# Two transformer blocks on one core: gain vectors by ScalarE's queue, the first weights in quarters, and three changes of order

## The chip, the core and the metric

One core of a Trainium2 chip runs the whole program in one launch. TensorE multiplies matrices and writes PSUM, VectorE, ScalarE and GpSimd (POOL in the profile) work on SBUF and, but for GpSimd, on PSUM; SyncE (SP) and ScalarE (ACT) issue transfers, each on a queue of its own. The engines run their own instruction streams in order and meet in semaphores. The metric is the device time of one execution in microseconds, the median of several.

## The reference

A layer on 256 tokens of width 1024, in fp32, made of two blocks. The first:

```python
h = rms_norm(x, g_norm); proj = h @ w_in        # q_a k_a v_a q_i k_i w_i z_a c_q c_kv k_rope z_b q_m z_m gates
o_a = dsa_attention(q_a, k_a, v_a, q_i, k_i, w_i)         # 8 heads of 64, the 64 best keys of an index score
o_b = causal_attention(q_b, k_b, v_b)                     # 8 heads of 96, from the latents c_q, c_kv
o_m = softmax(q_m @ k_m.T) @ v_m                          # 4 heads of 128, keys and values: rms_norm(mem) @ w_mem_kv
x = x + (sum_n sigmoid(gate_n) * ((o_n * silu(z_n)) @ w_branch[n])) @ w_out
```

The second block has three residual steps: a mixer (differential attention "DA", 4 heads, beside a chunked gated linear attention "GLA", whose inputs are `q * e_pos`, `q * e_neg` and `k * exp(L_end - L)`, both through w_o), a cross attention "C" of 4 heads of 256 over a second memory (w_cq, w_ckv, w_co), and a mixture of 32 experts, two for each token, with w_e_gate, w_e_up and w_e_down (201 MB of weights in all).

## The kernel before, in words

Everything is written out by hand: each engine's stream is one function body, and the order in it is the schedule. Tokens lie in two tiles of 128 (`t`), a width of 1024 in 8 slices of 128 (`k`).

**Weights** come in chunks of up to 2 MB. `chunks` lists them; SyncE's stream (from L1148) issues them in this order into a ring of three slots, each behind the last product that read the slot (`wait_full`, L1157). Ahead of the first chunk it issues mem, the nine `gains` (small vectors that all end in one 55 x 128 tile GR) and the positions. The first chunk, mk, is split into two halves; TensorE waits for the first on `first_landed`, for the rest before slice 4. The 20 vectors of `small` follow the fourth chunk. After the last chunk come the router's weights and the experts' stream: 96 loads of 2 MB into eleven places, each behind the work that frees its place (L1180 to L1212); from load 13 on every second one goes by ScalarE's queue (L1679).

**Projections.** `project` (L513) and `project_t` multiply a turned activation by a chunk, 512 or 256 columns at a time; an fp32 matmul shows as two records. `project_blocks` (L646) multiplies by blocks with 7 products in place of 8 (28 matmuls); GpSimd's `weight_sums` (L1302) makes the four sums of weight blocks for it, S_a, S_b, then w21 and w12 in place, four instructions each, and VectorE's `combine` (L1845) adds the products up as `block_products` counts them. `project_rows` (L553) does one token tile and half at a time. The argument `after` is a function that is called behind every matmul and may put other work there.

**Transposes.** `turn` (L576) transposes four 128 x 128 pieces through an AUX bank of PSUM; ScalarE (`drain_turned`, L1426) or, with a gain, VectorE (`drain_rows`, L1752) takes them out. There are four AUX banks; `wait_drained` waits until a bank was taken out. At the start (L722 to L732) TensorE transposes three tiles of mem, then GR, then the fourth, waits for all four drains and starts mk.

**Attention.** `attend` on TensorE, `soften` on ScalarE and `attention` on VectorE run the same steps s = 0, 1, ...: in step s TensorE computes the scores of unit s, transposes the probabilities of unit s-2 and multiplies unit s-3 by the values; VectorE masks unit s (scaling and row maximum), normalizes unit s-1 and takes the output of unit s-3; ScalarE does the exponentials of unit s, then copies the transposed probabilities of unit s-2. `spread` (L685) lays TensorE's steps evenly between the matmuls of a projection: all eleven steps of the first attention, "A" with 8 units, lie in chunk zb, behind its seventh matmul; qm follows. ScalarE does tanh of zb, VectorE `silu_t` of zb, behind their last step of A.

**GLA.** GpSimd's stream (from L1368) runs the weight sums of gv and ckv1, waits for the decays' exponentials, makes the three products QP, QN and KE (L1374 to L1376, counted by `gla_products`) and then the weight sums of gg. TensorE waits for `gla_products` behind gg, before it transposes KE; ScalarE waits for it before the tanh of gg.

**Cross attention.** wcq is computed in four pieces (t, h) (L921 to L938). For each ScalarE squares and drains the bank, VectorE norms it. TensorE transposes the keys xk ahead of piece (1, 0) and the queries of tile 0 ahead of (1, 1). ScalarE drains xk and the first queries behind its drain of piece (1, 0). `start_sum` (L940) adds x3 into an ACC bank through the identity, half by half; then come the four units of C and the output weights wco (`add_wco`), whose results let the last loads of the experts' first groups go (`x3_done`).

## Time and profile before

| | us |
|---|---|
| runs (3), lowest, median, highest | 1123.66, 1124.64, 1125.01 |
| the profiled execution | 1124.0 |
| its span | 1122.2 |
| TensorE busy, share of the span | 925.8, 83% |
| VectorE busy | 404.1, 36% |
| GpSimd busy | 247.3, 22% |
| ScalarE busy | 170.3, 15% |
| HBM read | 288.51 MB |

Times in the views count from the span's start. TensorE's busy time is that of its records, whose ends are modelled. "PEclk" is the clock granted to TensorE as a share of the full 2.4 GHz. An idle time in brackets stands before an instruction, with what ended it behind the arrow.

### The profile page before, as it was taken

What the parts mean: (1) busy time and instruction counts of PE and PEld (TensorE: products, weight loads), DVE (VectorE), ACT (ScalarE), POOL (GpSimd) and SP (SyncE); (2) the same over time, 40 slices, a digit from 0 to 9 for tenths busy, and PEclk for the clock granted to TensorE, in tenths of its full rate; (3) what the DMA queues carried; (4) which work ended last, traced back from release to release, by engine and by line L of the source; (5) the groups of instructions that cost most, each with busy time, mean ns of one, the idle gap of its engine ahead of it and who ended that gap; (6) DMA issues with size and microseconds to landing.
All of it is one profiled execution on the core that took longest, in us unless ns stands there. A gap on an engine that the chain in (4) does not pass through costs nothing.

```text
span 1122.2 us, 12455 instructions
## 1 busy us (share of the span) xinstructions
PE 925.8 (83%) x5006; PEld 581.2 (52%) x5006; DVE 404.1 (36%) x984; ACT 170.3 (15%) x370; POOL 247.3 (22%) x368
## 2 busy tenths in 40 slices
PE   6999999999999999989999999655656557473847
PEld 3775487789999878865544555221211213131312
DVE  5537935762223655866545424010000101010101
ACT  2114232431001003013312311000000000000000
POOL 4543141234753948930000000000000000000000
PEclk9999999999999999999999999887786978687889
DMA  7636242224445344524219458999999999999997
GB/s 281 195 121 225 80 145 76 76 76 150 154 170 208 109 152 155 203 93 150 79 71 350 180 225 371 425 429 428 428 428 428 426 428 428 428 428 428 429 421 276
DMA packets 64312, 290.38 MB, mean 259 GB/s; under 512 B 9015, under 2 KB 11902, under 8 KB 52222
## 3 DMA queue, kind: packets, MB, share of 16 engines
q1 hardware_dynamic: 58206, 205.16, 47.6%
q10 hardware_dynamic: 6048, 84.41, 17.7%
q8 instruction: 41, 0.67, 0.2%
q14 instruction: 17, 0.14, 0.0%
HBM read 288.51 MB, written 1.05 MB: 258 GB/s over the span
## 4 chain that ended last, share of the span: by engine, by line
PE 56%; DMA 29%; DVE 5%; POOL 5%; ACT 2%; issue 2%; SPq 1%; another core or an unknown queue 1%; DVEq 0%; ACTq 0%; POOLq 0%
PE ACC L530 11%; DMA ring<-in_w_e_down_dram 10%; DMA PJ<-in_w_e_down_dram 10%; PE ACC L545 8%; PE ACC L668 7%; PE ACC L671 7%; PE ACC L569 5%; DMA BIG<-in_w_e_gate_dram 4%; DMA ring<-in_w_e_gate_dram 4%; POOL ring L1298 4%; PE AUX L1097 4%; PE AUX L1061 3%; PE ACC L953 2%; PE AUX L580 2%; PE AUX L700 1%
## 5 line engine op out<-in xcount | busy, mean ns | idle before, releaser
L1298 POOL TENSOR_TENSOR ring<-ring 128x256 f32<-128x256 f32 x272 | 204.5, 782 | 173.7 <-PE ACC L668 72.4
L1061 PE MATMUL AUX<-ring,R 128*32 128x512 f32 x400 | 132.7, 716 | 41.8 <-DMA BIG<-in_w_e_up_dram 20.7
L545 PE MATMUL ACC<-BIG,ring 128*128 128x256 f32 (+1 forms) x464 | 106.2, 382 | 0.0
L545 PEld LDWEIGHTS ACC<-BIG,ring 128*128 128x128 f32 (+1 forms) x464 | 84.6, 187 | 15.6 <-issue 3.6
L2305 DVE SCALAR_TENSOR_TENSOR GB<-GB,AUX 128x512 f32<-128x512 f32 x8 | 5.5, 688 | 235.0 <-ACT GB L1683 235.0
L1061 PE MATMUL AUX<-R 128*32 128x512 f32 x176 | 60.7, 707 | 25.6 <-DMA ring<-in_w_e_up_dram 11.0
L1061 PE MATMUL AUX<-BIG,R 128*32 128x512 f32 x176 | 64.0, 737 | 20.3 <-DMA PJ<-in_w_e_up_dram 20.3
L1097 PE MATMUL AUX<-ring,BIG 128*32 128x512 f32 x160 | 60.2, 707 | 21.9 <-DMA R<-in_w_e_down_dram 12.3
L530 PE MATMUL ACC<-ring,BIG 128*128 128x512 f32 (+2 forms) x192 | 76.0, 554 | 0.0
L1061 PE MATMUL AUX<-SQE,R 128*32 128x512 f32 x112 | 61.6, 713 | 16.9 <-DMA ring<-in_w_e_up_dram 9.8
L1061 PEld LDWEIGHTS AUX<-ring,R 128*32 128x32 f32 x400 | 31.4, 129 | 76.0 <-issue 76.0
L671 PE MATMUL ACC<-ring 128*128 128x256 f32 x288 | 64.2, 380 | 5.0 <-POOL ring L1298 4.1
L530 PE MATMUL ACC<-ring,R 128*128 128x512 f32 (+1 forms) x136 | 59.9, 589 | 3.2 <-DVE R L1758 2.1
L671 PEld LDWEIGHTS ACC<-ring 128*128 128x128 f32 x288 | 54.5, 190 | 13.5 <-POOL ring L1298 4.9
L1061 PE MATMUL AUX<-PJ,R 128*32 128x512 f32 x160 | 51.1, 697 | 7.0 <-DMA ring<-in_w_e_up_dram 7.0
L569 PE MATMUL ACC<-ring,BIG 128*128 128x512 f32 x128 | 55.8, 592 | 0.0
L2307 DVE SCALAR_TENSOR_TENSOR GB<-GB,AUX 128x512 f32<-128x512 f32 x8 | 8.4, 1049 | 129.9 <-PE AUX L1061 129.9
L530 PEld LDWEIGHTS ACC<-ring,BIG 128*128 128x128 f32 x192 | 36.2, 190 | 36.2 <-issue 28.4
L1097 PE MATMUL AUX<-PJ,BIG 128*32 128x512 f32 x128 | 45.0, 724 | 11.4 <-DMA ring<-in_w_e_down_dram 11.4
L668 PE MATMUL ACC<-ring 128*128 128x128 f32 x384 | 44.7, 275 | 0.0
L668 PEld LDWEIGHTS ACC<-ring 128*128 128x128 f32 x384 | 44.1, 192 | 0.2
L671 PE MATMUL ACC<-ring,R 128*128 128x256 f32 x184 | 42.2, 388 | 0.0
(345 smaller groups left out, 1422.3 us busy)
## 6 DMA issues: line engine op xcount, KB each, us to landing
ring<-in_w_in_dram SPq DMA_DIRECT2D x20, 2048.0 KB, 7.9
ring<-in_w_e_gate_dram SPq DMA_DIRECT2D x8, 2048.0 KB, 39.2
ring<-in_w_e_up_dram SPq DMA_DIRECT2D x6, 2048.0 KB, 41.9
ring<-in_w_e_gate_dram ACTq DMA_DIRECT2D x6, 2048.0 KB, 27.8
ring<-in_w_e_down_dram SPq DMA_DIRECT2D x5, 2048.0 KB, 40.1
ring<-in_w_e_up_dram ACTq DMA_DIRECT2D x5, 2048.0 KB, 24.2
ring<-in_w_ckv_dram SPq DMA_DIRECT2D x4, 2048.0 KB, 8.1
BIG<-in_w_e_down_dram SPq DMA_DIRECT2D x4, 2048.0 KB, 21.7
```

The source lines that it names most:

```text
L530: mm = nc.tensor.matmul(bank[:, t * 512:t * 512 + width], lhs[:, i, t * P:(t + 1) * P], w[:, i, a:a + width], start=(i == 0), stop=(i == k ...
L545: mm = nc.tensor.matmul(bank[0:m, j * S:(j + 1) * S], w[:, i, a + j * P:a + j * P + m], rhs[:, i, :], start=(i == 0), stop=(i == k - 1))
L569: mm = nc.tensor.matmul(bank[:, c:c + 512], lhs[:, i, t * P:(t + 1) * P], w[:, i, :], start=(i == order[0]), stop=(i == order[-1]))
L580: mm = nc.tensor.transpose(bank[0:src.shape[1], j * P:(j + 1) * P], src, ident[:, :])
L668: mm = nc.tensor.matmul(bank[:, j * P:(j + 1) * P], left[:, k, j * P:(j + 1) * P], right[:, k, :], start=(k == 0), stop=(k == 3))
L671: mm = nc.tensor.matmul(bank, right[:, k, :], left[:, k, :], start=(k == 0), stop=(k == 3))
L700: return lambda o, t, h, i, nk: nc.tensor.matmul(o, queries(t, h, i), keys(h, i, nk), start=True, stop=True)
L953: mm = nc.tensor.matmul(ACC[t][:, h * 512:(h + 1) * 512], XT3[:, i, t * P:(t + 1) * P], slot_of(f"wco{h}")[:, i, :], start=False, stop=Fal ...
L1061: mm = nc.tensor.matmul(bank[r, :], M_xt[:, k, r], w[e][:, k, :], start=(k == 0), stop=(k == KD - 1))
L1097: mm = nc.tensor.matmul(AUX[2 + h][r, :], M_hidt[:, k, r], w[e][:, k, h * 512:(h + 1) * 512], start=(k == 0), stop=(k == 3))
L1298: ins = g.tensor_tensor(out[:, k, :], a[:, k, :], b[:, k, :], op)
L2307: v.scalar_tensor_tensor(out=permuted, in0=M_gated.rearrange("q (p k) -> q p k", k=4), scalar=0.5, in1=AUX[3][:, :].rearrange("q (p k) -> ...
```

## The change

Only the order, the queues and the split of one load change; the arithmetic stays.

- The nine gain vectors and the positions are issued by ScalarE's queue, at the head of its stream, instead of SyncE's between mem and mk.
- mk's first half is loaded in two parts of two slices each, with a semaphore each.
- TensorE transposes the gains first, then all of mem, and mk waits for a mem drain only ahead of the four slices that need it.
- Steps 0 to 5 of the first attention are spread over zb, steps 6 to 10 lie behind matmuls 5, 10, 15, 20 and 25 of qm. ScalarE and VectorE do tanh and silu of zb behind their step 5, and VectorE combines qm in four parts between its later steps.
- GpSimd makes gg's weight sums ahead of the GLA products.
- In the cross attention ScalarE drains xk behind wcq's piece (0, 1); the second `start_sum` is done in halves, one ahead of the last queries' transposes and one behind unit 1's scores; and in attention C ScalarE copies the transposed probabilities ahead of the exponentials of the same step.

```diff
--- before.py
+++ after.py
@@ -208,7 +208,7 @@
         pos_landed = sem("pos_landed")
-        first_landed = sem("first_landed")
+        first_landed = [sem(f"first_landed{i}") for i in range(2)]
         x_landed = sem("x_landed")
@@ -513,9 +513,7 @@
-                if name == "mk":
-                    pe.wait_ge(first_landed, 16)
-                else:
+                if name != "mk":
                     wait_chunk(name)
@@ -523,8 +521,13 @@
                     for i in range(k):
-                        if (name, t, i) == ("mk", 0, 4):
-                            wait_chunk(name)
+                        if name == "mk":
+                            if i % 4 == 0:
+                                wait_drained(pe, ("mem", t, i // 4))
+                            if t == 0 and i in (0, 2):
+                                pe.wait_ge(first_landed[i // 2], 16)
+                            elif (t, i) == (0, 4):
+                                wait_chunk(name)
                         if ready and t == 0:
@@ -720,15 +723,13 @@
             pe.wait_ge(consts_ready, 1)
-            pe.wait_ge(mem_landed, 16)
-            for t, g in ((0, 0), (0, 1), (1, 0)):
-                turn(2 * t + g, ("mem", t, g))
-
             pe.wait_ge(gains_landed, 16 * len(gains))
...
             nc.tensor.transpose(bank[:, 0:GC_N], GR[:, :], ident[0:GC_N, 0:GC_N]).then_inc(full, 1)
-            turn(3, ("mem", 1, 1))
-            wait_turned("mem")
+            pe.wait_ge(mem_landed, 16)
+            for t in range(TT):
+                for g in range(2):
+                    turn(2 * t + g, ("mem", t, g))
             project("mk", R2T)
@@ -775,8 +776,9 @@
             tiles = [(name, t) for t in range(TT) for name in ("qa", "ka")]
-            project_t("zb", XT3, after=spread("A", 0, 11, begin=7, ready=tiles + ["va"]))
-            project_blocks("qm", XT3, T_x, x0_sums)
+            project_t("zb", XT3, after=spread("A", 0, 6, begin=7, ready=tiles + ["va"]))
+            project_blocks("qm", XT3, T_x, x0_sums,
+                           after=lambda done: attend("A", 5 + done // 5, 6 + done // 5) if done % 5 == 0 else None)
             pe.wait_ge(roped, 2)
@@ -937,11 +939,11 @@
-            def start_sum(t, last):
+            def start_sum(t, last, halves=range(2)):
                 wait_drained(pe, last)
...
                     wait_drained(pe, ("wo", t_))
-                for h in range(2):
+                for h in halves:
                     nc.tensor.matmul(ACC[t][:, h * 512:(h + 1) * 512], ident[:, :], X3[:, t, h * 512:(h + 1) * 512],
@@ -1005,10 +1007,11 @@
             attend("C", 0, 1)
+            start_sum(1 - first_sum, ("wcq", 1, 1), [0])
             pe.wait_ge(heads_normed, 13)
             turn(3, ("xq", 1, 1))
-            start_sum(1 - first_sum, ("wcq", 1, 1))
             attend("C", 1, 2)
+            start_sum(1 - first_sum, ("wcq", 1, 1), [1])
             wait_turned("xq")
@@ -1148,10 +1151,6 @@
             sp.dma_start(R1v, rows(A["mem"])).then_inc(mem_landed, 16)
-            for dst, src in gains:
-                sp.dma_start(dst, src).then_inc(gains_landed, 16)
-            sp.dma_start(pos_i[:, :], A["positions"][0].rearrange("(t p) -> p t", p=P),
-                         allow_slow_non_contiguous=True).then_inc(pos_landed, 16)
             for c, (name, width, parts) in enumerate(chunks):
@@ -1159,7 +1158,8 @@
                     if c == 0:
-                        sp.dma_start(dst[:, 0:4, :], src[:, 0:4, :]).then_inc(first_landed, 16)
+                        for i in range(2):
+                            sp.dma_start(dst[:, 2 * i:2 * i + 2, :], src[:, 2 * i:2 * i + 2, :]).then_inc(first_landed[i], 16)
                         dst, src = dst[:, 4:KD, :], src[:, 4:KD, :]
@@ -1370,11 +1370,11 @@
                 weight_sums(name)
+            weight_sums("gg")
             pool.wait_ge(decay_e, 1)
...
             g.tensor_tensor(KE, kt(GK, 2), kt(EE, 2), ALU.mult).then_inc(gla_products, 1)
-            weight_sums("gg")
@@ -1436,10 +1436,21 @@
-            def soften(name, a=0, b=None):
+            def soften(name, a=0, b=None, drain_first=False):
+
+                def take_turned(s):
+                    u = first_unit[name] + s - 2
+                    nk = keys_of(units[name][s - 2][0])
+                    n = nk if name == "DA" else 2 * nk
+                    bank = wait_full(act, ("T", u))
+                    if u >= 2:
+                        wait_full(act, ("O", u - 2))
+                    a_.activation(buf(PT, u)[:, 0:n], bank[:, 0:n], ACT.Copy).then_inc(free_sem(("T", u)), 1)
...
                 for s in range(a, U + 2 if b is None else b):
+                    if s >= 2 and drain_first:
+                        take_turned(s)
                     if s < U:
@@ -1449,16 +1460,14 @@
                         last.then_inc(exped, 1)
-                    if s >= 2:
-                        u = first_unit[name] + s - 2
-                        nk = keys_of(units[name][s - 2][0])
-                        n = nk if name == "DA" else 2 * nk
-                        bank = wait_full(act, ("T", u))
-                        if u >= 2:
-                            wait_full(act, ("O", u - 2))
-                        a_.activation(buf(PT, u)[:, 0:n], bank[:, 0:n], ACT.Copy).then_inc(free_sem(("T", u)), 1)
-
-
+                    if s >= 2 and not drain_first:
+                        take_turned(s)
+
+
+            for dst, src in gains:
+                act.dma_start(dst, src).then_inc(gains_landed, 16)
+            act.dma_start(pos_i[:, :], A["positions"][0].rearrange("(t p) -> p t", p=P),
+                          allow_slow_non_contiguous=True).then_inc(pos_landed, 16)
             act.wait_ge(consts_ready, 1)
@@ -1527,8 +1536,9 @@
                 drain_turned(("ka", t), KT4, 4)
-            soften("A")
+            soften("A", 0, 6)
             tanh_of("zb", ZT[:, 1024:2048])
+            soften("A", 6)
             wait_drained(act, "qm")
@@ -1637,15 +1647,16 @@
                     drain(key, [(CQN[:, t, h * 512:(h + 1) * 512], lambda b: b[:, 0:512])])
-                    if (t, h) == (1, 0):
+                    if (t, h) == (0, 1):
                         for k in range(TT):
...
                                 drain_turned(("xk", k, g), CK8[:, 4 * g:4 * g + 4, :], 4)
+                    if (t, h) == (1, 0):
                         for g in range(2):
...
                 drain_turned(("xq", 1, g), CQ8[:, 4 * g:4 * g + 4, :], 4)
-            soften("C")
+            soften("C", drain_first=True)
@@ -2032,9 +2043,16 @@
             silu_t("za", ZT[:, 0:1024])
-            attention("A")
+            attention("A", 0, 6)
             silu_t("zb", ZT[:, 1024:2048])
-            combine("qm", by_rows(PJ3, PJ_QM))
+            attention("A", 6, 7)
+            combine("qm", by_rows(PJ3, PJ_QM), range(0, 1))
+            attention("A", 7, 9)
+            combine("qm", by_rows(PJ3, PJ_QM), range(1, 2))
+            attention("A", 9, 10)
+            combine("qm", by_rows(PJ3, PJ_QM), range(2, 3))
+            attention("A", 10)
+            combine("qm", by_rows(PJ3, PJ_QM), range(3, 4))
             norm_heads(SQ[:, 0:1024], 8, 128,
...
             attention("B")
```

## Rows read from the trace of the kernel before

**Rows 1.** The page, span in 40 slices: TensorE busy (tenths), then GB/s.
```profile
PE   6999999999999999989999999655656557473847
...
GB/s 281 195 121 225 80 145 76 76 76 150 154 170 208 109 152 155 203 93 150 79 71 350 180 225 371 425 429 428 428 428 428 426 428 428 428 428 428 429 421 276
```

**Rows 2.** Chain of waits: start us, length us, engine, tile, line, instructions.
```profile
0.82 5.04 DMA R<-in_mem_dram
6.00 2.79 PE AUX L580 x12
...
9.37 2.50 DVE R L1758 x4
...
12.16 15.67 PE ACC L530 x32
...
691.53 20.75 DMA PJ<-in_w_e_down_dram
```

**Rows 3.** Windows: stretch, length, busy us (x instructions), PEclk, DMA share, GB/s.
```profile
13.00:15.00 2.00, 2.00 (x4) 0.88 (x3) 1.10 (x7) 0.00 (x0) 0.00 (x0) 0.50 1.02 401
655.00:666.00 11.00, 11.00 (x34) 5.33 (x33) 3.11 (x13) 2.42 (x6) 0.00 (x0) 1.00 0.08 34
666.00:676.00 10.00, 9.58 (x40) 5.12 (x38) 3.26 (x15) 3.25 (x4) 0.00 (x0) 1.00 0.57 211
684.00:700.00 16.00, 16.00 (x149) 6.47 (x149) 5.56 (x19) 0.60 (x1) 0.00 (x0) 1.00 1.01 428
```

**Rows 4.** Timeline of SyncE's queue, start and seam: start us, length us, line.
```profile
4.01 0.27 SPq L1152 DMA_DIRECT2D SQE<-in_norm_ffn_dram  x1
4.32 0.40 SPq L1153 DMA_DIRECT2D pos_i<-in_positions_dram  x1
4.76 0.47 SPq L1162 DMA_DIRECT2D ring<-in_w_mem_kv_dram  x1
...
675.61 0.33 SPq L1206 DMA_DIRECT2D ring<-in_w_e_down_dram  x1
```

**Rows 5.** DMA issues: loads, KB each, median us from issue to landing.
```profile
ring<-in_w_e_gate_dram SPq DMA_DIRECT2D x8, 2048.0 KB, 39.2
...
ring<-in_w_e_gate_dram ACTq DMA_DIRECT2D x6, 2048.0 KB, 27.8
...
GB<-in_cross_q_norm_dram SPq DMA_DIRECT2D x1, 128.0 KB, 8.0
...
pos_i<-in_positions_dram SPq DMA_DIRECT2D x1, 1.0 KB, 2.9
```

**Rows 6.** Windows: zb with qm, then wcq's third piece to wco.
```profile
153.85:197.65 43.80, 39.95 (x226) 32.53 (x225) 23.11 (x57) 14.95 (x46) 7.90 (x12) 1.00 0.27 95
611.44:640.66 29.22, 25.19 (x102) 16.42 (x102) 16.12 (x47) 12.12 (x31) 0.00 (x0) 1.00 0.63 247
```

**Rows 7.** Timeline of the first attention: VectorE, TensorE, ScalarE, VectorE.
```profile
178.58 0.69 DVE L1807 TENSOR_REDUCE SMALL<-SQE 128x2 f32<-128x512 f32 x1
...
181.02 0.41 PE L619 MATMUL AUX<-ident,SQE 128*128 128x128 f32 x2 [1.34 <-ACT BIG L1459]
...
184.98 1.03 ACT L1524 ACTIVATE BIG<-ACC 128x1024 f32<-128x1024 f32 x1 [0.83 <-PE ACC L545]
...
186.20 1.22 DVE L1897 SCALAR_TENSOR_TENSOR BIG<-BIG,ACC 128x1024 f32<-128x1024 f32 x1
```

**Rows 8.** Timeline of GpSimd around the GLA products, and TensorE in gg.
```profile
426.30 41.45 POOL L1298 TENSOR_TENSOR ring<-ring 128x256 f32<-128x256 f32 x52 [5.05 <-PE ACC L671]
467.83 1.33 POOL L1374 TENSOR_TENSOR PJ<-BIG 128x512 f32<-128x512 f32 x1
...
471.57 9.16 POOL L1298 TENSOR_TENSOR ring<-ring 128x256 f32<-128x256 f32 x8
...
483.69 3.69 PE L671 MATMUL ACC<-ring 128*128 128x256 f32 x16 [0.90 <-issue]
```

**Rows 9.** Timeline of TensorE in the cross attention.
```profile
613.35 1.12 PE L580 MATMUL AUX<-ident,R 128*128 128x128 f32 x8 [1.76 <-ACT R L1420]
```

## The prediction

> **What bounds the kernel now.** The slices of the page come first [rows 1]: in the first 21 of 40 TensorE is busy and the transfers move 71 to 281 GB/s; from slice 26 on they move 428 GB/s and hardly vary. So the last 40% is a stream of expert weights, and everything before it is a matter of when that stream can start. The chain of waits says the same [rows 2]: its first transfer is mem (0.82 to 5.86), the next is the down weights at 691.53, and between the two its pieces are TensorE, VectorE, ScalarE and GpSimd. No weight load in between is waited for. At the seam the windows show 34 GB/s in 655 to 666 us, 211 in 666 to 676, 428 from 684 on [rows 3]: the loads there are released by TensorE's work on x3 (SyncE's queue issues one at 675.61 [rows 4]), not held up by bandwidth. Whatever TensorE reaches earlier before 675.61 therefore arrives in full at the end, because the bytes behind that point and their rate stay the same. That is the rule of my sum: four stretches, what each takes off TensorE's path, added.
>
> **1. Start.** Now: SyncE issues mem, then nine gain vectors (the last at 4.01) and the positions, then the first mk weights at 4.76 [rows 4]. Mem is transposed three tiles deep (6.00 to 8.79), then the gains, VectorE copies them and only then drains the four tiles (9.37 to 11.87); mk's 32 records start at 12.16 and take 15.67 us [rows 2]. Their first four are 0.86 us apart, the others 0.43 (4 x 0.86 + 28 x 0.43 = 15.5): the clock granted in 13 to 15 us is 0.50, the lower of its two levels, 1.2 GHz [rows 3]. Changed: the gains go by ScalarE's queue, TensorE transposes them first, then 16 pieces of mem, and mk starts when the first drain is done.
> The gains' landing G is what decides. ScalarE does nothing until mem lands at 5.86, so its ten issues of about 0.3 us (SyncE's: nine gains between 1.3 and 4.3 [rows 4]) cover 0.8 to 3.9 us and delay nothing if its queue opens when SyncE's does; the ninth gain is out at about 3.4. From issue to landing the trace has no small load on this queue. Bounds: 2.9 us (the positions, on a quiet queue) and 8.0 us (a 128 KB gain load behind weights) [rows 5], so G is 6.3 to 11.4. I take 6.4, near the positions, whose kilobyte is the nearest in size. Then: gains transposed until 6.7; 16 transposes at 2.79/12 = 0.23 us each until 10.4; VectorE's copy and first drain (0.23 + 0.62) end at about 8.4 under that cover, so mk starts at 10.4, 1.7 us earlier. It starts behind four unbroken microseconds of TensorE work, where today it starts behind a hole of 2.1 us, and I count it at the higher level: 16 x 0.86 = 13.7 us against 15.67, so 1.9 more. Less 0.2 for hand-overs: **3.4 us** (with G = 11.4 mk starts at 15.4 and ends at 29.2, a loss of 1.4; with transposes at half of 0.23, as the higher level would have them, and G = 5.5, a gain of 5.5).
> The quarters cost nothing: SyncE gains ten issues and pays one (0.5 us), the first half megabyte is out at 1.3 instead of 4.76, and at 401 GB/s (13 to 15 us [rows 3]) mem and two quarters are in by about 8, the whole of mk by 11; k = 4 is wanted at 13.8. The per-half waits on the drains cost nothing either: a drain takes 0.62, the four matmuls before its use 3.4. x and mv come earlier too. The positions are used only after mem's norm and sums, far behind either landing.
>
> A rule of the Trainium skill speaks against this part. DMA: Bandwidth & Descriptors, section Queues, rings and completion order, says that each DMA engine takes turns between its queues in packets, about 9 to 17 descriptors of one queue before the next gets its turn. By that, each gain vector could wait for a turn behind the large loads that now follow mem without a break. In the expert stream here both queues carry 2 MB loads and ScalarE's land sooner (27.8 us) than SyncE's (39.2) [rows 5], so the rows show no starving of that queue; nothing shows it for small ones.
>
> **2. First attention.** Its eleven steps sit in zb (32 matmuls of 0.43 us), qm follows without a step of it. In 153.85 to 197.65, both together, TensorE is busy 39.95 of 43.80 us [rows 6]. The idle 3.85 stands before transposes, in four gaps of 0.7 to 1.34 us, the last at 181.02 [rows 7]. Each of those transposes waits for VectorE's normalizing, which stands behind the next unit's masking (0.69 + 0.69 [rows 7]), or for ScalarE's copy, which stands behind the next exponentials. The modelled ends hide about 0.2 more in each of four gaps: 4.6 in all. Now steps 0 to 5 are spread over 25 matmuls of zb (4.2 matmuls, 1.8 us between steps instead of 1.0), 6 to 10 over qm (2.15 us). The extra 0.8 to 1.2 us covers gaps of 0.7 to 1.3. Late next is the crossing from zb to qm: ScalarE does tanh of zb (1.03 [rows 7]) before the copy of unit 4's transposes, VectorE the silu (1.22 [rows 7]) before masking unit 6. I step it through: zb ends at 0, step 5 is over at 1.8, unit 5's exponentials and copy at 4.2, tanh 5.3, silu 6.5, mask 6 at 7.4, copy of unit 4 at 8.7, while TensorE wants that bank at 8.3. Cost 0.4, other hand-overs 0.3. **3.9 us** (bounds: 0 if the crossing eats it, 4.6). VectorE's combine of qm is cut into four parts between the steps, but its last part still follows qm's last product, so the normalizing of qm that opens the next attention keeps its distance. Masking takes no more work.
>
> **3. GLA products.** GpSimd is the path from 426.30: 52 sums until 467.8, products 467.83 to 471.57 (three of 1.25), then gg's 16 sums, the first eight in 9.16; TensorE waits for them, starts on the third operand at 483.69 and, with 24 records of 0.215 left, is through gg at 488.9, where it transposes KE [rows 8]. Changed: gg's sums start at 467.83. Until 471.5 VectorE only combines and the sums go at 0.8 each (41.45/52), four and a half of them; beside VectorE's long multiplications, until 480.1, they took 1.15, so seven and a half more until then; the last four, with VectorE idle, at 0.7 until 482.9. TensorE: third operand at 480.1 instead of 483.69, gg through at 485.5. But KE is wanted right there, and the products now run 482.9 to 486.65. So TensorE goes on at 486.75 instead of 488.9: **2.2 us**, not the 3.7 moved (bounds: 3.4 if the products run faster, and -1.1 if all 16 sums run at 1.15, which ends them at 486.2 and the products at 489.9). ScalarE's tanh of gg waits for the products as well; today it follows gg, then it follows both. No transfer is moved here.
>
> **4. Cross attention.** wcq's third piece ends at 611.44 and the first wco matmul starts at 640.66; of 29.22 us TensorE is busy 25.19 [rows 6]. Holes: 1.76 before the first queries' transposes ([rows 9]; their bank holds xk, which ScalarE drains only behind its drain of wcq's third piece, 0.6 + 0.6 us first), the rest of the 4.03 at the last norm and in the softmax; with 0.2 of modelled end in six places 5.2 in all. Changed: xk is drained after the second piece, under the third: the 1.76 goes, the norms of the first queries are long done. The last piece ends at 619.4, its norm at 624.2 (4.8 after, as today); TensorE has 4.7 us until there, with only half of the second sum (0.86) moved in front of it: 0.1 idle. VectorE masks unit 0 at 624.2 and no longer stands behind S(1): normalized at 628.9, when TensorE has just put S(1), half a sum and S(2) behind it at 629.0. Copies ahead of exponentials free the bank for T(1) at 630.2; T(1) waits 0.3 for its norm, T(2) 0.2. That leaves 1.1 of 5.2: **4.1 us** (bounds: 1.5, if only the first hole goes, to 5.2). Late next is VectorE's masking, 1.4 a unit. SyncE's loads here are released by TensorE and move along.
>
> **Sum.** 3.4 + 3.9 + 2.2 + 4.1 = 13.6 us. The profiled execution took 1124.0 with a span of 1122.2; it gives 1110.4. The median is 1124.64, 0.6 more: 1111.0.
>
> **Rivals.**
> (a) The gains land late, G = 11.4: start -1.4 instead of +3.4, total 8.8 gained, 1115.8. For it: the large loads now share the engines with them; against it: 2.9 us for the positions behind mem.
> (b) One of parts 2 or 4 yields nothing, because VectorE's or ScalarE's order makes the next hole: 9.6 gained, 1115. For it: in part 2 two engines are within half a microsecond of being late.
> (c) The end does not follow: the stream is bound by bytes that could not start sooner, 1124.6. Against it: 34 GB/s in 655 to 666 [rows 3].
> (d) Slower: the gains starve. Mem, mk, x, mv and cq, 7.8 MB at 400 GB/s from 2.2 us, keep the engines until about 21.7; if the gains come through only behind them, at 22.6, TensorE, which now waits for the gains before its first transpose, starts mk at 26.6 and, at the lower clock first, ends it at 42.1 instead of 27.8. Price 14.3 against the 10.2 of the other parts: 1128.7. It decides once G passes 18.5. This is where the page's turn-taking would lead at its worst, one gain vector a turn.
>
> **How the numbers follow.** Forecast 0.62 (its own range 1107.5 to 1113.5), (a) 0.14, (b) 0.13, (c) 0.04, (d) 0.04, more than forecast by warm transposes 0.03. A measurement of this kernel tells 0.2%, 2.2 us, from no change. The range goes to 1106.5 below and to 1118 above, past (a) and (b). Faster 0.92, same 0.04, slower 0.04.
>
> **What would show it.** Start: mk's first record at about 10.4, no records 0.86 apart, its end near 24.2. First attention: TensorE busy over 98% in zb and qm together, about 40 us for both instead of 43.8. GLA: a TensorE hole of about 1.2 us before KE's transposes, the products last on GpSimd. Cross: from the end of wcq's third piece to the first wco matmul 25 us. The 428 GB/s plateau begins 13 to 14 us earlier and lasts as long. I am wrong if TensorE's first record comes after 8 us, if a hole of more than 1 us stands in qm, or if the plateau starts earlier and the end does not.

## The result

The kernel after takes 1115.29 us, the median of four runs (1113.73 to 1115.91), against 1124.2 for the kernel before beside it (four runs, 1123.66 to 1125.01): ratio 0.9918, 95% interval 0.9905 to 0.9931, or 9.2 us less (7.8 to 10.7; here and below (1 - ratio) x 1124). Forecast were 1111.0 and 13.6 us less, with a range to 1118.0. The profiled execution took 1115.91, its span is 1114.1; before: 1124.0 and 1122.2.

TensorE at the start of the kernel after (timeline: start us, us, engine, line, operation, tiles, count, in brackets the idle time before it and what ended it):

```profile
9.18 0.32 PE L728 MATMUL AUX<-ident,SQE 55*128 55x55 f32 x1 [9.18 <-DMA SQE<-in_norm_ffn_dram]
9.44 3.67 PE L583 MATMUL AUX<-ident,R 128*128 128x128 f32 x16
12.90 14.14 PE L533 MATMUL ACC<-ring,R 128*128 128x512 f32 x32
26.88 1.91 PE L583 MATMUL AUX<-ident,BIG 128*128 128x128 f32 x16
...
37.42 3.72 PE L674 MATMUL ACC<-ring 128*128 128x256 f32 x16 [1.73 <-ACT R L1481]
...
42.71 3.71 PE L533 MATMUL ACC<-ring,BIG 128*128 128x384 f32 x11
```

These answer to [rows 2]. The first record comes at 9.18, when the ninth gain vector has landed. mk starts at 12.90, later than before's 12.16, and behind its first record all stand 0.43 us apart (in before the first four stand about 0.86 apart), so its last one makes way for x's transposes at 26.88 (before 27.67). Then a hole that before does not have: 1.73 us ahead of mv's second bank. cq starts at 42.71; in before it started at 41.50.

The same stretch on ScalarE and VectorE (timelines of the kernel after; "R L1481" is the drain of mk, L1744, L1747 and L1756 are steps of x's norm), then x's norm in the kernel before:

```profile
4.30 0.45 ACTq L1468 DMA_DIRECT2D SQE<-in_norm_ffn_dram  x1
16.32 1.06 ACT L1404 ACTIVATE BIG<-BIG 128x1024 f32<-128x1024 f32 x1 [6.87 <-DVE SMALL L1919]
20.13 0.16 DVE L1747 SCALAR_TENSOR_TENSOR NW<-NW 128x2 f32<-128x2 f32 x1
20.32 0.71 DVE L1744 TENSOR_TENSOR NW<-NW 128x2 f32<-128x2 f32 x1
22.43 2.31 DVE L1756 TENSOR_SCALAR BIG<-BIG,RS 128x1024 f32<-128x1024 f32 x2
...
35.96 0.26 ACT L1476 ACTIVATE PJ<-PJ 128x64 f32<-128x64 f32 x1 [16.15 <-DVE PJ L1938]
36.12 1.25 ACT L1481 ACTIVATE R<-ACC,SMALL 128x512 f32<-128x512 f32 x2
```

```profile
19.99 1.42 DVE L1745 TENSOR_SCALAR BIG<-BIG,RS 128x1024 f32<-128x1024 f32 x2
```

Mem's drains end 2 us later than before, and so does mem's norm. The squares of x now wait for it and start at 16.32; in before they waited for x itself and started at 15.40, so that is 0.9 us of delay. The end of x's norm now falls beside GpSimd's weight sums (from 20.30): the last three two-element instructions take 0.65 to 0.71 instead of 0.16, and the two long ones 2.31 instead of 1.42. That is 2.4 us more, and x's norm ends 3.3 us late in all, at 24.7. The rotary angles end at 35.9 (before 33.1), and ScalarE's stream has the Sin that needs them ahead of the drain of mk, whose bank has been full since 27.0 and is the one mv's second half wants.

The other three parts, TensorE in the kernel after unless it says otherwise (first attention, GLA, cross attention):

```profile
152.98 1.91 PE L583 MATMUL AUX<-ident,PJ 128*128 128x128 f32 x16
...
186.99 0.41 PE L622 MATMUL AUX<-ident,SQE 128*128 128x128 f32 x2 [1.03 <-ACT BIG L1448]
...
195.42 1.91 PE L583 MATMUL AUX<-ident,R 128*96 128x128 f32 x16
...
481.50 1.27 POOL L1377 TENSOR_TENSOR PJ<-BIG 128x512 f32<-128x512 f32 x1
482.82 0.66 PE L850 MATMUL AUX<-ident,PJ 128*128 128x128 f32 x4 [1.80 <-POOL PJ L1377]
...
630.32 3.60 PE L955 MATMUL ACC<-ring,BIG 128*128 128x512 f32 x8
```

The windows of the two stretches of [rows 6] in the kernel after (length, then busy us of PE, PEld, DVE, ACT and POOL, granted clock, DMA share, GB/s):

```profile
154.73:195.42 40.69, 39.63 (x227) 32.45 (x226) 23.27 (x57) 14.84 (x46) 12.00 (x18) 1.00 0.29 102
605.38:630.32 24.94, 24.36 (x102) 16.27 (x100) 16.17 (x47) 10.40 (x27) 0.00 (x0) 1.00 0.73 293
```

zb and qm together: 40.69 us instead of 43.80 ([rows 6]). The four holes under zb ([rows 7] has the last) are gone; one of 1.03 stands in qm, which starts at 175.90. GLA: KE's transposes at 482.82 instead of 488.94, while the sums ahead of them start at 422.65 instead of 426.30 ([rows 8]): 2.47 gained. Cross: 24.94 us from the queries' transposes to wco; in before it is 29.06 to the same record (640.50 in this view; the window of [rows 6] ends at 640.66), so 4.1 gained, and the 1.76 us of [rows 9] are gone.

At the seam SyncE issues the first half-load of down weights at 678.49 instead of 688.10, 9.6 us earlier (its queue, in the kernel before and in the kernel after):

```profile
688.10 0.33 SPq L1212 DMA_DIRECT2D PJ<-in_w_e_down_dram  x1
```

```profile
678.49 0.33 SPq L1212 DMA_DIRECT2D PJ<-in_w_e_down_dram  x1
```

Along the way the lead is -0.9 ahead of zb, 2.2 behind qm (3.1 won), 3.6 at gr's first product (1.4 more, by no part of the change), 6.1 behind GLA, 10.2 at wco, and 9.6 at the seam; ahead of the seam, in 669 to 671 us, the granted clock is 0.50 in the kernel after and 1.00 in the kernel before. The span ends only 8.1 earlier.

### The profile page after: what moved, and what is told of

Same layout as the page of the kernel before. It is cut to its first block, busy times and chain, and to the rows that moved or that the text cites. A ratio compares the mean times of both kernels' runs of the same rounds, so it can differ in the third digit from the quotient of the medians.

```text
span 1114.1 us, 12457 instructions
## 1 busy us (share of the span) xinstructions
PE 925.4 (83%) x5006; PEld 582.2 (52%) x5006; DVE 406.4 (36%) x984; ACT 170.5 (15%) x370; POOL 248.3 (22%) x368
## 4 chain that ended last, share of the span: by engine, by line
PE 56%; DMA 28%; DVE 6%; POOL 5%; ACT 2%; issue 2%; another core or an unknown queue 1%; ACTq 0%; SPq 0%; DVEq 0%; POOLq 0%
PE ACC L533 10%; DMA R<-in_w_e_gate_dram 9%; PE ACC L548 9%; PE AUX L1064 7%; PE ACC L671 7%; PE ACC L572 5%; POOL ring L1298 5%; PE ACC L674 4%; DMA ring<-in_w_e_gate_dram 4%; DMA SQE<-in_w_e_gate_dram 4%; DMA PJ<-in_w_e_up_dram 4%; DMA ring<-in_w_e_up_dram 4%; PE ACC L955 2%; PE AUX L583 2%; DMA PJ<-in_w_e_down_dram 2%; PE AUX L1100 2%
## 5 line engine op out<-in xcount | busy, mean ns | idle before, releaser
L1100 PE MATMUL AUX<-ring,BIG 128*32 128x512 f32 x160 | 64.5, 741 | 21.9 <-DMA R<-in_w_e_down_dram 12.3
L1064 PE MATMUL AUX<-SQE,R 128*32 128x512 f32 x112 | 61.5, 713 | 16.9 <-DMA ring<-in_w_e_up_dram 10.7
L674 PEld LDWEIGHTS ACC<-ring 128*128 128x128 f32 x288 | 54.3, 190 | 11.1 <-ACT R L1481 2.1
L1100 PE MATMUL AUX<-PJ,BIG 128*32 128x512 f32 x128 | 45.0, 732 | 13.5 <-DMA ring<-in_w_e_down_dram 13.5
```

Source lines behind the costliest of these rows:

```text
L674: mm = nc.tensor.matmul(bank, right[:, k, :], left[:, k, :], start=(k == 0), stop=(k == 3))
L1064: mm = nc.tensor.matmul(bank[r, :], M_xt[:, k, r], w[e][:, k, :], start=(k == 0), stop=(k == KD - 1))
L1100: mm = nc.tensor.matmul(AUX[2 + h][r, :], M_hidt[:, k, r], w[e][:, k, h * 512:(h + 1) * 512], start=(k == 0), stop=(k == 3))
```

## Experiments

All kernels were timed in five rounds beside the kernel before. "Part alone" kernels are the kernel before with one of the four parts; the others are the kernel after with edits.

| kernel | median us | ratio to before, 95% | us less |
|---|---|---|---|
| Start alone | 1123.55 | 1.0003 [0.9994, 1.0012] | -0.3 (-1.3 to 0.7) |
| first attention alone | 1120.57 | 0.9972 [0.9963, 0.9981] | 3.1 (2.1 to 4.2) |
| GLA alone | 1121.63 | 0.9983 [0.9974, 0.9992] | 1.9 (0.9 to 2.9) |
| cross alone | 1119.49 | 0.9965 [0.9951, 0.9978] | 3.9 (2.5 to 5.5) |
| all but Start | 1114.02 | 0.9915 [0.9901, 0.9928] | 9.6 (8.1 to 11.1) |
| after, again | 1114.24 | 0.9911 [0.9896, 0.9926] | 10.0 (8.3 to 11.7) |
| after, mk drained before Sin | 1113.22 | 0.9904 [0.9889, 0.9920] | 10.8 (9.0 to 12.5) |
| after, mem turned first | 1112.57 | 0.9900 [0.9886, 0.9915] | 11.2 (9.6 to 12.8) |
| both | 1111.88 | 0.9895 [0.9880, 0.9910] | 11.8 (10.1 to 13.5) |
| both, TensorE kept busy | 1112.65 | 0.9898 [0.9882, 0.9913] | 11.5 (9.8 to 13.3) |
| both, combine later | 1110.91 | 0.9884 [0.9867, 0.9900] | 13.0 (11.2 to 14.9) |
| after, busy tail | 1114.98 | 0.9918 [0.9905, 0.9932] | 9.2 (7.6 to 10.7) |

### The parts one by one

My theory from the trace: Start gives nothing, the others about what was forecast. The rival is the forecast itself. Each kernel is before with the hunks of one part of the diff shown above, as for GLA:

```diff
+            weight_sums("gg")
             pool.wait_ge(decay_e, 1)
...
             g.tensor_tensor(KE, kt(GK, 2), kt(EE, 2), ALU.mult).then_inc(gla_products, 1)
-            weight_sums("gg")
```

> The kernel before with the Start part alone (norm vectors issued by ScalarE, first weights in quarters, the gains' transpose ahead of the four memory tiles). As forecast: 3.4 us less, 1120.8. By what the trace of after shows: mk ends 0.8 us earlier, but x's norm (VectorE L1722 to L1745) ends about 3 us later, with it the trig angles, ScalarE's Sin and the drain of mk behind it; TensorE has a hole of 1.7 us ahead of mv's second bank, cq begins 1.2 us later than in before, and 0.9 us of that is left at 111 us: 1125.1 (1124.5 to 1126).

> The kernel after without its Start part (first attention, GLA and cross attention as in after; start as in before). If Start costs 0.9 us: 1115.3 - 0.9 = 1114.4, and cq begins at 41.7. If Start gives what I forecast for it: 1115.3 + 3.4 = 1118.7. Where the clock at 395 to 404 us (1.00 in after, 0.79 to 0.87 in before) belongs to the parts kept here, gr begins 3.7 - 0.9 = 4.6 us or more ahead of before; where it belongs to Start, 3.4.

> The kernel before with the first-attention part alone (steps 5 to 10 beside qm's products instead of all beside zb's). As forecast: 3.9 us less than before. By the trace of after: 3.1 less from zb's first product to qm's last (43.8 us becomes 40.7), because one hole of about 1.0 us behind ScalarE stays where zb ends. Rival: the gain is taken back by what follows (VectorE's combines of qm now stand between attention steps), less than 1.5.

> The kernel before with the GLA part alone (gg's weight sums on GpSimd ahead of the three products). As forecast: 2.2 us less; by the trace of after 2.45 less, with a hole of 1.8 us on TensorE ahead of KE's transposes. Rival: nothing, where the stage is not on the path that sets the end.

> The kernel before with the cross-attention part alone (wcq's sums by halves, ScalarE's drain ahead of the exponentials). Forecast and trace of after agree: 4.1 us less between wcq's third piece and wco, the plateau and the end 4.1 earlier. Rival: the end gains 2.6 only, since TensorE's low clock in the last group gives back 1.5, as in after's profiled run.

TensorE in the kernel with Start alone, and behind it in the kernel with all but Start:

```profile
37.36 3.72 PE L674 MATMUL ACC<-ring 128*128 128x256 f32 x16 [1.44 <-ACT R L1479]
...
42.64 3.71 PE L533 MATMUL ACC<-ring,BIG 128*128 128x384 f32 x11
```

```profile
9.56 1.12 PE L580 MATMUL AUX<-ident,R 128*128 128x128 f32 x4 [0.39 <-DVE GC L1912]
12.33 16.70 PE L530 MATMUL ACC<-ring,R 128*128 128x512 f32 x32 [1.65 <-DVE R L1767]
...
42.70 1.78 PE L530 MATMUL ACC<-ring,BIG 128*128 128x384 f32 x5
```

A window of the kernel with the first attention alone, which has before's start, and the same of the kernel after (columns as above; both read 1.00 as granted clock):

```profile
13.00:15.00 2.00, 2.00 (x4) 0.69 (x3) 1.19 (x8) 0.00 (x0) 0.00 (x0) 1.00 1.01 395
```

```profile
13.00:15.00 2.00, 2.00 (x6) 0.95 (x6) 1.65 (x8) 0.00 (x0) 0.00 (x0) 1.00 1.02 407
```

Start is worth nothing that these runs can tell: 0.3 us more alone (-0.7 to 1.3), where the forecast was 3.4 less, and taking it out of after leaves 9.6 less against 9.2 and 10.0 with it. I had expected a loss of 0.9 us. The times don't exclude it, but the second fence does not bear it out: with before's own start, cq begins at 42.70 here, not at the 41.7 expected. In the five profiles with that start it begins at 41.50, 42.14, 42.44, 42.70 and 42.99 (mean 42.4). What varies is how long TensorE runs at half its rate: in 13 to 17 us it has 8 records in before's profile, 6 in each of the other four, and 10 in the kernel after. The granted clock of 13 to 15 us is 0.50 in before ([rows 3]) but reads 1.00 in the other four, with 3 or 4 records, as few as before's 4, where the kernel after has 6. There the first transposes of mem are at half rate too (12 in 2.79 us, where 16 take 1.91 later on), so the spacing of the records, not that column, shows the low level; before's profile holds the shortest stretch of it. With the new start cq begins at 42.71, 42.64, 42.93 and 42.70. A loss of 1.2 us, which one pair of profiles showed, is one of 0.4 over nine. And the 0.4 are a difference of two larger numbers: mk ends 1.7 us earlier on average, and 2.1 are lost between there and cq, most of it in the hole.

The other three hold. From the transposes ahead of zb to those behind qm first attention alone takes 42.43 us, after 42.44, before 45.55. GLA alone: 425.56 to 485.77, 2.43 us less than before. Cross alone: from the queries' transposes (610.69) to wco (635.63) 24.94 us, the same as after. The medians agree, and their sum with Start, 3.1 + 1.9 + 3.9 - 0.3 = 8.6 us, lies inside the interval of the whole.

```profile
187.59 0.41 PE L619 MATMUL AUX<-ident,SQE 128*128 128x128 f32 x2 [1.03 <-ACT BIG L1460]
```

```profile
485.77 0.66 PE L848 MATMUL AUX<-ident,PJ 128*128 128x128 f32 x4 [1.81 <-POOL PJ L1377]
```

```profile
635.63 3.60 PE L953 MATMUL ACC<-ring,BIG 128*128 128x512 f32 x8
```

### The hole ahead of mv's second bank

```diff
-            act.wait_ge(trig_arg, 2)
-            a_.activation(trig[:, 128:192], trig[:, 64:128], ACT.Sin).then_inc(trig_ready, 1)
...
             drain_mem("mk", 0)
+            act.wait_ge(trig_arg, 2)
+            a_.activation(trig[:, 128:192], trig[:, 64:128], ACT.Sin).then_inc(trig_ready, 1)
```

> The kernel after with one edit on ScalarE: the drain of mk stands ahead of the Sin instead of behind it. If the hole of 1.73 us ahead of mv's second bank is ScalarE's queue order (mk's bank is full at 27.0, the Sin can't run before VectorE's angles at 35.96): the hole goes, cq begins at 41.1 instead of 42.9, and the time falls by 1.7 us to 1113.6. Rival: VectorE, whose sums of mv's products start only at 38.4, is late next, cq begins at 42.3 or later, and the time falls by 0.6 at most. Second rival: the drain stands beside VectorE's work and slows it, no gain.

```profile
32.16 7.07 PE L674 MATMUL ACC<-ring 128*128 128x256 f32 x32
...
41.10 5.08 PE L533 MATMUL ACC<-ring,BIG 128*128 128x384 f32 x15
```

The hole is gone and cq begins at 41.10, the number of the theory; VectorE's combine, the rival, costs 0.3 us at most (cq starts 2.03 us behind the start of mv's last eight records, in after 1.73). What was won holds: qm's transposes come at 193.89, 1.5 ahead of after. The time of the whole (10.8 us less; the kernel after had 9.2 and 10.0) points the same way without telling it apart.

### TensorE's order at the start

```diff
+            pe.wait_ge(mem_landed, 16)
+            for t, g in ((0, 0), (0, 1), (1, 0)):
+                turn(2 * t + g, ("mem", t, g))
             pe.wait_ge(gains_landed, 16 * len(gains))
...
-            pe.wait_ge(mem_landed, 16)
-            for t in range(TT):
-                for g in range(2):
-                    turn(2 * t + g, ("mem", t, g))
+            turn(3, ("mem", 1, 1))
```

> The kernel after with TensorE's order at the start as in before (three memory tiles turned ahead of the gains), ScalarE's order unchanged. Of the 2.4 us that both edits gave, by theory most is this one's: mk ends about 0.4 us earlier than in after, but x's norm and the trig angles on VectorE end 2.3 us earlier (33.6 instead of 36.0), and ScalarE's drain of mk with them: no hole ahead of mv's second bank, cq at 40.5 to 41.0, 1.8 to 2.3 us under after. Rival: the two edits each take one half, 1.0 to 1.2 under after.

> The kernel after with two edits at the start: ScalarE drains mk ahead of the Sin, and TensorE turns three memory tiles ahead of the gains, as in before (gains still issued by ScalarE, weights still in quarters). Theory: after's mk begins late (12.9) because all four turns stand behind gains that land at 9.05; with three of them ahead mk begins at 10.6 to 11.0, as my forecast had it, and x's norm ends 1 to 2 us earlier. If the clock stays full mk ends at 25.0 and the time is 1.9 us under the one-edit kernel (drain first): 1111.3 to 1111.8 on the scale where after is 1115.3. Rival: TensorE idles between its turns and mk, the granted clock is 0.50 for the first 3 us as in before, mk ends at 26.3 to 26.5 and 0.5 us is gained. Second rival: VectorE, slower beside GpSimd's sums of mv's weights from 20.3, takes it back: no gain.

TensorE with this edit alone, then with both (below it VectorE's norm of x):

```profile
10.52 15.13 PE L533 MATMUL ACC<-ring,R 128*128 128x512 f32 x32
...
35.75 3.72 PE L674 MATMUL ACC<-ring 128*128 128x256 f32 x16 [1.45 <-ACT R L1481]
...
41.03 5.32 PE L533 MATMUL ACC<-ring,BIG 128*128 128x384 f32 x16
```

```profile
10.49 16.22 PE L533 MATMUL ACC<-ring,R 128*128 128x512 f32 x32
...
40.38 5.97 PE L533 MATMUL ACC<-ring,BIG 128*128 128x384 f32 x18
19.61 1.42 DVE L1756 TENSOR_SCALAR BIG<-BIG,RS 128x1024 f32<-128x1024 f32 x2
```

mk now starts at 10.5, as forecast, and x's norm ends 3.7 us earlier with both (21.0 against 24.7), ahead of most of GpSimd's sums. With the edit alone the hole stays (1.45 us; I had expected it gone, but mk ends earlier too and TensorE is back at the bank by 34.3) and cq begins at 41.03, 1.7 earlier; with both it begins at 40.38, 2.3 earlier. mk takes 15.1 and 16.2 us instead of 14.1, since its first products are at half rate again: the first rival of the second expectation. But no wait for drains stands between the last turn and mk here, only short pauses earlier on (0.26 and 0.38 us). So the hole of 2.1 us ahead of mk, which the prediction made answerable for the low clock, is not needed for it. What the late order has and this one has not is that mk starts only at 12.7 to 13.1, behind sixteen transposes without a pause. In time both edits give 11.8 us less, 1.0 more than the drain alone, where the theory asked for 1.9 and its rival for 0.5.

### Keeping TensorE busy, at the start and at the end

At the start (nine idle products in all, `keep_busy(5)` ahead of the wait for mem, 2 and 2 around the last turn), and in the last group of experts:

```diff
+            def keep_busy(n):
+                for _ in range(n):
+                    nc.tensor.matmul(ACC[1][:, 0:512], zeros_h[:, :], ones_h[:, :].unsqueeze(1).broadcast_to([P, 4, P]),
+                                     start=True, stop=True)
...
+                if g == GROUPS - 1:
+                    for _ in range(20):
+                        nc.tensor.matmul(AUX[0][:, :], zeros_h[:, :], ones_h[:, :].unsqueeze(1).broadcast_to([P, 4, P]),
+                                         start=True, stop=True)
                 expert_rows(AUX[3], g, 1, moe_up)
```

> The kernel with both start edits and nine idle bfloat16 products on TensorE (5 before the memory rows land, 2 while the gains are copied, 2 ahead of mk; no result uses them). Asked is the low clock at the start: in the kernels that turn the memory tiles at 6 us the granted clock is 0.50 from 9.5 us on, for 3 to 5 us, and mk takes 15.7 to 17.0 us instead of 14.1. Theory: it is low since TensorE stood idle before; busy from 4.9 us it stays at 1.00, mk ends at 24.4, VectorE's combine of mv is late next, cq begins at 38.9 to 39.3, 1.2 to 1.5 us under the kernel with both edits. Rival: the low stretch only moves, as the tail's did when idle products were put there: no difference. Second rival: x's norm or GpSimd's sums of mv's weights (31.1) hold TensorE back and the gain is below 0.5.

> The kernel after with 20 idle bfloat16 products on TensorE (they write a free bank, no result uses them) between the last group's gate products and its up products. In after the plateau begins 9.6 us earlier than in before, the span ends 8.1 earlier. Theory: the missing 1.5 us are TensorE's clock in the last group (0.50 at 1080 to 1088 and 0.65 at 1096 to 1100; in before 0.50 at 1092 to 1096 and 1.00 from 1100), which makes TensorE and not the last row of weights end last. Then the last down products wait for the last row, and the time falls by 1.0 to 1.5 us, to 1114. Rival: the last rows' landing sets the end anyway, or the 1.5 us are the spread between executions: 1115.3, no difference. Second rival: the 20 products end after the up weights have landed and cost up to 2 us.

> The kernel after once more, unchanged, beside the kernels of this group. What varies between executions is asked: in its first profile the stream's plateau began 9.6 us ahead of before and the span ended 8.1 ahead. Theory: the 1.5 us are the last group's low TensorE clock, which differs between executions; a second profile ends 433.7 to 435.6 us after SyncE issues the first half-load of the down weights (before and all experiments lie there), and the ratio to before is 0.9918 again. If the loss belongs to the change, it is 435.6 again.

TensorE at the start of the first, then windows of the last group in the kernel after and in the one with the busy tail (the number ahead of the last two is the granted clock):

```profile
10.98 13.90 PE L533 MATMUL ACC<-ring,R 128*128 128x512 f32 x32
...
39.80 6.37 PE L533 MATMUL ACC<-ring,BIG 128*128 128x384 f32 x19 [1.09 <-DVE R L1888]
```

```profile
1078.00:1082.00 4.00, 0.00 (x0) 0.00 (x0) 0.00 (x0) 0.00 (x0) 0.00 (x0) 0.54 0.97 399
1082.00:1086.00 4.00, 3.42 (x17) 0.94 (x21) 0.00 (x0) 0.00 (x0) 0.00 (x0) 0.50 1.03 410
1086.00:1090.00 4.00, 4.00 (x32) 1.21 (x28) 0.00 (x0) 0.00 (x0) 0.00 (x0) 0.68 1.03 410
...
1094.00:1098.00 4.00, 3.42 (x22) 1.39 (x25) 0.69 (x1) 0.38 (x1) 0.00 (x0) 0.68 1.03 410
```

```profile
1078.00:1082.00 4.00, 2.12 (x10) 0.78 (x8) 0.00 (x0) 0.00 (x0) 0.00 (x0) 1.00 0.97 407
1082.00:1086.00 4.00, 2.23 (x19) 0.85 (x22) 0.00 (x0) 0.00 (x0) 0.00 (x0) 0.88 1.01 405
1086.00:1090.00 4.00, 4.00 (x32) 1.37 (x28) 0.00 (x0) 0.00 (x0) 0.00 (x0) 0.69 1.03 412
...
1094.00:1098.00 4.00, 3.42 (x22) 1.29 (x24) 0.69 (x1) 0.38 (x1) 0.00 (x0) 0.66 1.03 410
```

At the start mk now takes 13.9 us, all of it at the full rate. The expectation names a granted clock of 0.50 for the kernels with the early turns; but for before's, their windows read 1.00 there, and it is the spacing of the records that is doubled. VectorE's combine of mv is late next, as expected; cq begins at 39.80, 0.6 earlier, not 1.2. In the time nothing is left of it (11.5 and 11.8 less).

At the end the idle products gave no time, though they changed the clock: in 1078 to 1082 us, where TensorE had idled, it is 1.00 instead of 0.54, then 0.88 instead of 0.50. The rest of the spell stayed (0.69 and 0.68), and so did the next one at 1094. That after's profile ends 1.5 us late is not the change's: from the issue of the first half-load of down weights to the end of the span it took 435.6 us, in its second profile 434.4, in before 434.1, in the others 433.7 to 435.1. I can't say from these runs when the clock falls, nor that it makes the 1.5 us: after's first profile had two low spells in the last group and its second one, but the profile with the busy tail had two as well and took 434.3.

### The hole where zb ends

```diff
-            attention("A", 6, 7)
+            attention("A", 6, 8)
             combine("qm", by_rows(PJ3, PJ_QM), range(0, 1))
-            attention("A", 7, 9)
+            attention("A", 8, 9)
```

> The kernel with both start edits, and with VectorE's first part of qm's combine one attention step later (behind step 7 instead of behind step 6). Asked is the one hole of 1.0 us that after keeps where zb ends, the 0.8 us by which my forecast for the first attention was too high. Theory: it is the two combine instructions (0.80 us, 183.03 to 183.83 in after) that stand ahead of the masking of unit 7; behind them come ScalarE's exponentials and its copy of unit 5, for which TensorE waits. Then the hole falls to 0.2 and the stretch from zb's transposes to qm's last product from 42.43 us to 41.6. Rival: the tanh and the silu of zb (1.0 and 1.2 us) make it, the hole stays at 1.0. In the time of the whole, 0.8 us can't be told: 1111 to 1112.

The hole in question stands in qm, 11 us behind its first product, and not at the end of zb itself. VectorE in the kernel after around it, then TensorE in the edited kernel:

```profile
183.03 0.42 DVE L1872 COPY PJ<-ACC 128x256 f32<-128x256 f32 x1
183.49 0.42 DVE L1873 TENSOR_TENSOR PJ<-ACC,PJ 128x256 f32<-128x256 f32 x1
183.83 0.68 DVE L1814 SCALAR_TENSOR_TENSOR SQE<-AUX,BIG 128x512 f32<-128x512 f32 x1
```

```profile
150.79 1.91 PE L583 MATMUL AUX<-ident,PJ 128*128 128x128 f32 x16
183.99 0.41 PE L622 MATMUL AUX<-ident,SQE 128*128 128x128 f32 x2 [0.23 <-ACT BIG L1448]
192.43 1.91 PE L583 MATMUL AUX<-ident,R 128*96 128x128 f32 x16
```

The hole falls from 1.03 to 0.23 us, the stretch from 42.44 to 41.64: the theory holds, and its rival, the tanh and the silu, is out. This is also the fastest kernel, 1110.91 us, with an interval that ends at 0.9900 where that of after begins at 0.9905 in one group of runs and at 0.9896 in the other; from the kernel with both start edits its time can't be told.

## Why the prediction was right or wrong

- **What bounds the kernel: right.** The load at the seam is issued 9.6 us earlier and the end moves along, but for the 1.5 us that come and go between executions.
- **Start, 3.4 forecast, 0 measured: the failed step.** Two of its terms were wrong and the third was priced right for a reason that does not hold. (1) G, the gains' landing, taken as 6.4, was 9.05: the ninth issue is out at 4.30, not 3.4, and landed 4.75 us later beside 390 GB/s, not 2.9. I took the positions' landing on a quiet queue and had written 11.4 as the other bound; in the kernel after the positions themselves took 6.6. As all sixteen transposes of mem stood behind it, mk began at 12.90 instead of 10.4. By the prediction's own sum that leaves 0.75 of the 3.4, and mk did end 0.8 earlier than in before's profile. (2) I followed TensorE only to mk's end. Behind the later drains of mem come mem's norm, x's squares, x's norm, the angles, the Sin and ScalarE's drain of mk, and mv's second bank wants that drain: 1.4 to 2.1 us of hole in four profiles. The drains also came late enough to push x's norm under GpSimd's sums. The text names none of this; the squares' wait for mem's norm and the Sin ahead of the drain both stand in the code. (3) The low clock was there to be removed, and was: mk took 13.9 to 14.5 us in five profiles instead of 15.7 to 17.0, 2.3 on average where 1.9 was forecast. But the price came from one profile, the mildest of five, and the reason given, the hole ahead of mk, fell with the early turns. Two of my own signs of being wrong were met: TensorE's first record after 8 us, and a hole of more than 1 us in qm. mk's end was far from 24.2, and TensorE was busy for 97.4% of zb and qm, not for over 98%.
- In the seven profiles in which TensorE waited for the nine small loads on the second queue, its record behind them came at 8.9 to 9.4 us, about 5 us from the last issue, while large loads filled the first queue. Rival (d), one gain a turn, did not happen. On the Trainium skill's page DMA: Bandwidth & Descriptors, section Queues, rings and completion order: waiting turn by turn behind the other queue's packets, as the section has it, fits a landing later than on a quiet queue; no run here tests it.
- **First attention, 3.9 forecast, 3.1 measured: right mechanism, one term mis-sized.** The four holes under zb went. "Combine is cut into four parts between the steps" I had costed at nothing; its first part stands ahead of a masking and costs the 0.80 us that are missing: with it one step later the hole is 0.23.
- **GLA, 2.2 forecast, 2.47 measured: right.** The sums run as stepped through (products end at 482.77; forecast 486.65 less the 3.65 gained before, 483.0); the hole is 1.8 rather than 1.2.
- **Cross, 4.1 forecast, 4.1 in the traces, 3.9 by the medians: right.**
- **The sum.** 3.4 too much for Start and 0.8 for the crossing: 13.6 - 4.2 = 9.4, measured 9.2. Rival (a), a late G, gave 1115.8, half a microsecond from the measured time, but that is luck: G was 9.05 and not 11.4, and the rest of the loss came from the hole at mv and from the combine in qm, which it does not hold. The 9.6 us at the seam are not a clean check of the sum either: 1.4 of them are the clock's and no part of the change, and about half a microsecond went the other way ahead of the seam.

## What to carry to other kernels

When an operation that feeds one engine is delayed by even two microseconds, follow each of the other engines from it to the next buffer that they share with the first, not only the path of the engine that you watch. A drain that waits for nothing belongs ahead of an instruction that waits for another engine. And take a term of one or two microseconds, when it rests on a low clock, from several profiles of the same code: here one pair of profiles called a part 1.2 us slower that is neutral. Read the level from the spacing of the records as well as from the granted clock, which read 1.00 over products at half rate in four profiles.

## What the runs showed of the hardware

TensorE's low clock comes in spells that a kernel does not decide alone. From the transposes behind qm to the first product of gr (the projection at 400 us) all fourteen profiles are of the same code; nine profiles take 204.5 us and five take 205.7 to 205.9 (before, after's second, mk drained first, and the two with idle products). In 390 to 400 us each of the five has a window of 5 us with a granted clock of 0.66 to 0.79, and each of the nine reads 1.00. These are the 1.4 us between the first two profiles. The windows of the two profiles of the kernel after show it, same code, one with and one without:

```profile
395.00:400.00 5.00, 4.58 (x27) 3.85 (x26) 4.90 (x12) 0.00 (x0) 3.55 (x2) 1.00 0.01 2
```

```profile
395.00:400.00 5.00, 5.00 (x24) 4.59 (x23) 4.07 (x10) 0.00 (x0) 2.53 (x1) 0.69 0.01 2
```

The Trainium skill, TensorE: Matmul & The Clock Gate, Part 1, says that the number of cold matmuls at a kernel's start differs from run to run with the phase of the clock's monitor. The five profiles with before's start agree: mk takes 15.7 to 17.0 us in them, for the same 32 records.

GpSimd's weight sums slow VectorE's smallest instructions most, as a share: in the kernel after 0.16 us alone, 0.65 to 0.71 beside them; a normalizing of 1024 columns takes 0.71 alone and 1.16 beside them. With the early turns x's norm is through its small instructions before the sums start, and they keep their 0.16. The Trainium skill, SBUF — State Buffer, section Who interferes with whom, has the second of the two engines, where they contend, wait until the first's instruction is over. The trace agrees: 0.65 to 0.71 is near the length of one of GpSimd's sums in that stretch (0.72 us).
